# One attention branch's masked softmax: where its mask is added, and the order of its steps

## The reference, cut to what matters

```python
p_c = masked_softmax(jnp.einsum('bqghd,bcgd->bghqc', qn, kc_blk), cmp_end[None, :] <= t[:, None])
o_c = jnp.einsum('bghqc,bcgd->bqghd', p_c, vc_blk)
...
def masked_softmax(s, mask):
    s = jnp.where(mask, s, -jnp.inf)
    m = jnp.max(s, axis=-1, keepdims=True)
    m = jnp.where(jnp.isfinite(m), m, 0.0)
    e = jnp.exp(s - m)
    den = jnp.sum(e, axis=-1, keepdims=True)
    return e / jnp.where(den > 0.0, den, 1.0)
```

## Time and profile before

| what | value |
|---|---|
| median of 3 runs | 2557.27 us (2555.11 to 2559.82) |
| profiled execution | 2556.63 us, of which the traced span is 2554.8 us |
| PE busy | 2360.6 us (92%) |
| DVE / ACT / POOL busy | 1002.7 / 739.9 / 160.7 us |
| mean granted TensorE clock | 0.935 of full speed |
| the stage of the change | 1913.5 to 1942.4 us of the span, about 29 us, 1.1% |

### The profile page before, as it was taken

One profiled execution on the slowest core, in us unless ns is written; L12 is line 12 of the kernel. 1 busy time (PEld: TensorE's weight loads), 2 busy tenths in 40 slices (PEclk: granted clock), 3 DMA queues, 4 the chain that ended last, 5 costly groups with the idle time before them and its releaser, 6 DMA issues. The chain is left out here.

```text
span 2554.8 us, 35043 instructions
## 1 busy us (share of the span) xinstructions
PE 2360.6 (92%) x15098; PEld 1797.8 (70%) x15098; DVE 1002.7 (39%) x1684; ACT 739.9 (29%) x1249; POOL 160.7 (6%) x195
## 2 busy tenths in 40 slices
PE   6999999889999999984889999999987998999997
PEld 3545555768888778884767888877855556788885
DVE  2022365343333338553134433423336662442333
ACT  2124212232222224222223422322103562431331
POOL 0004100000000000022000000000022440000000
PEclk8999999899999989985589999998996998999999
DMA  7140014012132122000021222212110004122210
GB/s 298 66 189 34 1 68 166 34 66 99 66 130 76 43 99 99 34 34 4 2 99 66 99 99 99 99 69 99 68 34 1 1 2 165 66 99 99 99 66 33
DMA packets 17130, 196.23 MB, mean 77 GB/s; under 512 B 2000, under 2 KB 3152, under 8 KB 5072
## 3 DMA queue, kind: packets, MB, share of 16 engines
q1 hardware_dynamic: 15824, 189.67, 20.0%
q10 hardware_dynamic: 1152, 4.32, 0.4%
HBM read 189.78 MB, written 2.10 MB: 75 GB/s over the span
## 5 line engine op out<-in xcount | busy, mean ns | idle before, releaser
L1701 DVE TENSOR_TENSOR wsp_mlp<-ring,wsp_mlp 128x1024 fp32r<-128x1024 f32 x128 | 156.8, 1225 | 438.2 <-ACT wsp_mlp L1663 438.2
L1663 ACT CAST wsp_mlp<-ring 128x1024 fp32r<-128x1024 f32 x128 | 134.3, 1049 | 349.4 <-PE psum L1648 345.0
L1645 PE MATMUL psum<-hs_mlp,wsp_mlp 128*128 128x512 f32 x512 | 201.6, 394 | 8.1 <-DVE hs_mlp L1534 8.1
L1645 PE MATMUL psum<-acts_mlp,wsp_mlp 128*128 128x512 f32 x512 | 202.4, 395 | 0.0
L1647 PE MATMUL psum<-hs_mlp,wsp_mlp 128*128 128x512 f32 x512 | 201.2, 393 | 0.0
L1648 PE MATMUL psum<-hs_mlp,wsp_mlp 128*128 128x512 f32 x512 | 201.0, 393 | 0.0
L1648 PE MATMUL psum<-acts_mlp,wsp_mlp 128*128 128x512 f32 x512 | 199.4, 389 | 0.0
L1647 PE MATMUL psum<-acts_mlp,wsp_mlp 128*128 128x512 f32 x512 | 199.3, 389 | 0.0
L1701 DVE TENSOR_TENSOR wsp_ffn<-ring,wsp_ffn 128x1024 fp32r<-128x1024 f32 x66 | 80.9, 1225 | 237.3 <-ACT wsp_ffn L1663 237.3
L427 PE MATMUL psum<-hsev,wspev 128*128 128x512 f32 x672 | 157.2, 397 | 3.9 <-DVE wspev L407 3.9
L427 PEld LDWEIGHTS psum<-hsev,wspev 128*128 128x128 f32 x672 | 128.9, 192 | 31.9 <-DVE wspev L407 4.7
(11 more groups left out here) (427 smaller groups left out, 3984.3 us busy)
## 6 DMA issues: line engine op xcount, KB each, us to landing
ring<-weights SPq DMA_DIRECT2D x85, 2048.0 KB, 8.1
ring<-weights SPq DMA_DIRECT2D x3, 1024.0 KB, 5.2
xT<-xin SPq DMA_DIRECT2D x2, 1024.0 KB, 6.8
cst<-consts ACTq DMA_DIRECT2D x1, 1921.0 KB, 13.5
ring<-weights SPq DMA_DIRECT2D x1, 1280.0 KB, 6.6
mixT<-ctxin ACTq DMA_DIRECT2D x1, 1024.0 KB, 15.4
ring<-weights SPq DMA_DIRECT2D x2, 512.0 KB, 3.6
arena<-arena_low SPq DMA_DIRECT2D x8, 128.0 KB, 2.3
```

The costliest lines, as they stand in the source:

```text
L1645: pe.matmul(tile_bank(g, j), w_hi, src[:, 0, k0 + i, :], start=(first and i == 0), stop=False)
L1663: act.copy(wsp[:, q % 2, 0, :], raw_view(q)).then_inc(s["w_hi"], 1)
L1701: dve.tensor_tensor(wsp[:, q % 2, 1, :], raw_view(q), wsp[:, q % 2, 0, :].bitcast(F32), ALU.subtract).then_inc(s["w_lo"], 1)
```

## The change

- PE starts each score bank with a matmul of the identity and the mask row (broadcast to 8 heads, 248 columns), `start=True`; the 16 score matmuls then accumulate onto it. A tile's two banks now lie side by side (2i and 2i + 1), and `cmp_tile(i)` reads both as one operand.
- DVE's four mask additions go. The maximum is taken from PSUM; a new small instruction lifts it to at least `NEG / 2`, so that a row that is masked whole gives exp of a very large negative number, that is zero, and the product with `cmp_ok` goes, with its table of constants. The subtraction reads PSUM and writes `pc`.
- DVE's order is now `less_max(0)`, `less_max(1)`, `share(0)`, `less_max(2)`, `share(1)`, `less_max(3)`, `share(2)`, `share(3)`, where `less_max` is maximum, floor and subtraction, and `share` all that follows the exponential.
- `pc` has four buffers, so the wait for the transposes goes. POOL zeroes column 31 alone; PE waits for it (`cs_edge`) ahead of its transposes.
- ACT's copies now stand between the exponentials: exp(0), exp(1), copy(0), exp(2), copy(1), exp(3), copy(2), copy(3). On PE all scores still stand ahead of all transposes.

The diff:

```diff
@@ -122,7 +122,6 @@
     end = np.arange(32)[None, None, :] * CMP_STRIDE + CMP_BLOCK - 1
     ok = (end <= t) & (np.arange(32)[None, None, :] < NB_CMP)
     out["cmp_neg"] = np.where(ok, 0.0, NEG).astype(f32).reshape(P, TT * 32)
-    out["cmp_ok"] = ok.astype(f32).reshape(P, TT * 32)
     out["eighth"] = np.full((P, 1), 0.125, f32)
     out["one"] = np.ones((P, 1), f32)
     return out
@@ -2662,75 +2661,95 @@
         n6.close()
 
 
-        pc = sb("pc", [P, 2, NH, 32], n3)
+        pc = sb("pc", [P, TT, NH, 32], n3)
         cst8 = sb("cst8", [P, TT, 4, NH], n3)
         n4 = ExitStack()
         pcT = hT[:, 0:4, :]
-        cs_done, cs_sub, cs_exp, cs_prob, cs_turn, cs_out = (
-            sem(n) for n in ("cs_done", "cs_sub", "cs_exp", "cs_prob", "cs_turn", "cs_out"))
+        cs_done, cs_sub, cs_exp, cs_prob, cs_turn, cs_edge = (
+            sem(n) for n in ("cs_done", "cs_sub", "cs_exp", "cs_prob", "cs_turn", "cs_edge"))
+
+        def eights(ap):
+            return ap.rearrange("p (a x) -> p a x", a=2)
+
+        def cmp_tile(i):
+            both = psum.rearrange("p (b a n) -> p b a n", a=2, b=4)[:, i, :, 0:256]
+            return both.rearrange("p a (x n) -> p a x n", n=32)[:, :, :, 0:31]
+
+        def cmp_probs(i):
+            return pc[:, i, :, 0:31].rearrange("p (a x) n -> p a x n", a=2)
+
         with nc.Block() as block:
             @block.tensor
             def _(pe):
-                def cmp_scores(i):
+                for i in range(TT):
+                    for a in range(2):
+                        shut = C("cmp_neg", 32 * i, 31).rearrange("p (o n) -> p o n", o=1).to_broadcast([P, 8, 31])
+                        pe.matmul(cmp_tile(i)[:, a], ident, shut, start=True, stop=False)
                     for h in range(NH):
                         g, j = h // 4, h % 4
                         rows = slice(64 * (g % 2), 64 * (g % 2) + 64)
 
-                        at = 512 * (i + 4 * (g % 2)) + (4 * (g // 2) + j) * 32
+                        at = 512 * (2 * i + g % 2) + (4 * (g // 2) + j) * 32
                         last = pe.matmul(psum[:, at:at + 31], qT[rows, 4 * (g // 2) + j, i * P:(i + 1) * P],
-                                         kcb[rows, (g // 2) * 31:(g // 2) * 31 + 31], start=True, stop=True)
+                                         kcb[rows, (g // 2) * 31:(g // 2) * 31 + 31], start=False,
+                                         stop=(g >= 2 and j == 3))
                     last.then_inc(cs_done, 1)
-                for i in range(TT):
-                    cmp_scores(i)
+                pe.wait_ge(cs_edge, 1)
                 for i in range(TT):
                     pe.wait_ge(cs_prob, i + 1)
                     for g in range(NG):
-                        last = pe.transpose(bank(i)[:, g * P:(g + 1) * P],
-                                            pc[:, i % 2, 4 * g:4 * g + 4, :].rearrange("p a b -> p (a b)"), ident)
+                        at = 8 * (g % 2) + 4 * (g // 2)
+                        last = pe.transpose(bank(2 * i)[:, g * P:(g + 1) * P],
+                                            pc[:, i, at:at + 4, :].rearrange("p a b -> p (a b)"), ident)
                     last.then_inc(cs_turn, 1)
+
+            @block.gpsimd
+            def _(pool):
+                pool.memset(pc[:, :, :, 31], 0.0).then_inc(cs_edge, 1)
 
             @block.vector
             def _(dve):
                 link = chain(dve, "cmp_chain")
-                link(dve.memset(pc[:, :, :, :], 0.0))
+
+                def col(i, k):
+                    return cst8[:, i, k, :]
+
+                def wide(i, k):
+                    return eights(col(i, k)).rearrange("p a (x o) -> p a x o", o=1).to_broadcast([P, 2, 8, 31])
+
+                def less_max(i):
+                    dve.wait_ge(cs_done, i + 1)
+                    link(dve.tensor_reduce(eights(col(i, 0)), cmp_tile(i), AX.X, ALU.max))
+                    link(dve.tensor_scalar(col(i, 0), col(i, 0), NEG / 2, None, ALU.max))
+                    dve.tensor_tensor(cmp_probs(i), cmp_tile(i), wide(i, 0), ALU.subtract).then_inc(cs_sub, 1)
+
+                def share(i):
+                    dve.wait_ge(cs_exp, i + 1)
+                    link(dve.tensor_reduce(eights(col(i, 1)), cmp_probs(i), AX.X, ALU.add))
+                    link(dve.tensor_scalar(col(i, 2), col(i, 1), 0.0, None, ALU.is_equal))
+                    link(dve.tensor_tensor(col(i, 1), col(i, 1), col(i, 2), ALU.add))
+                    link(dve.reciprocal(col(i, 2), col(i, 1)))
+                    by_head = gates[:, i, 0:48:3].rearrange("p (x a j) -> p a x j", a=2, j=4)
+                    link(dve.tensor_tensor(col(i, 3).rearrange("p (a x j) -> p a x j", a=2, j=4),
+                                           col(i, 2).rearrange("p (a x j) -> p a x j", a=2, j=4), by_head, ALU.mult))
+                    dve.tensor_tensor(cmp_probs(i), cmp_probs(i), wide(i, 3), ALU.mult).then_inc(cs_prob, 1)
+
+                less_max(0)
                 for i in range(TT):
-                    e = pc[:, i % 2, :, 0:31]
-
-                    def row(name, n=NH):
-                        return C(name, 32 * i, 31).rearrange("p (o n) -> p o n", o=1).to_broadcast([P, n, 31])
-
-                    def col(k):
-                        return cst8[:, i, k, :].rearrange("p (h o) -> p h o", o=1)
-                    dve.wait_ge(cs_done, i + 1)
-                    if i >= 2:
-                        dve.wait_ge(cs_turn, i - 1)
-                    for g in range(NG):
-                        s = bank(i + 4 * (g % 2))[:, 128 * (g // 2):128 * (g // 2) + P]
-                        last = dve.tensor_tensor(e[:, 4 * g:4 * g + 4, :],
-                                                 s.rearrange("p (h n) -> p h n", n=32)[:, :, 0:31],
-                                                 row("cmp_neg", 4), ALU.add)
-                    link(last)
-                    link(dve.tensor_reduce(cst8[:, i, 0, :], e, AX.X, ALU.max))
-                    dve.tensor_tensor(e, e, col(0).to_broadcast([P, NH, 31]), ALU.subtract).then_inc(cs_sub, 1)
-                    dve.wait_ge(cs_exp, i + 1)
-                    link(dve.tensor_tensor(e, e, row("cmp_ok"), ALU.mult))
-                    link(dve.tensor_reduce(cst8[:, i, 1, :], e, AX.X, ALU.add))
-
-                    link(dve.tensor_scalar(cst8[:, i, 2, :], cst8[:, i, 1, :], 0.0, None, ALU.is_equal))
-                    link(dve.tensor_tensor(cst8[:, i, 1, :], cst8[:, i, 1, :], cst8[:, i, 2, :], ALU.add))
-                    link(dve.reciprocal(cst8[:, i, 2, :], cst8[:, i, 1, :]))
-                    link(dve.tensor_tensor(cst8[:, i, 3, :], cst8[:, i, 2, :], gates[:, i, 0:48:3], ALU.mult))
-                    dve.tensor_tensor(e, e, col(3).to_broadcast([P, NH, 31]), ALU.mult).then_inc(cs_prob, 1)
+                    if i + 1 < TT:
+                        less_max(i + 1)
+                    share(i)
 
             @block.scalar
             def _(act):
                 for i in range(TT):
                     act.wait_ge(cs_sub, i + 1)
-                    e = pc[:, i % 2, :, 0:31]
-                    act.activation(e, e, ACT.Exp).then_inc(cs_exp, 1)
-                for i in range(TT):
-                    act.wait_ge(cs_turn, i + 1)
-                    act.copy(pcT[:, :, i * P:(i + 1) * P], bank(i).rearrange("p (g n) -> p g n", g=NG))
+                    act.activation(cmp_probs(i), cmp_probs(i), ACT.Exp).then_inc(cs_exp, 1)
+                    if i >= 1:
+                        act.wait_ge(cs_turn, i)
+                        act.copy(pcT[:, :, (i - 1) * P:i * P], bank(2 * i - 2).rearrange("p (g n) -> p g n", g=NG))
+                act.wait_ge(cs_turn, TT)
+                act.copy(pcT[:, :, (TT - 1) * P:TT * P], bank(2 * TT - 2).rearrange("p (g n) -> p g n", g=NG))
 
 
         n2.close()
```

## The result

The changed kernel is slower. Six runs of each: median 2568.52 us (2564.8 to 2571.56) against 2556.19 us (2554.14 to 2560.0); ratio 1.0046, interval 1.0033 to 1.0059. Both intervals say slower.

A forecast was written before the change was run, and what follows sets the result against it. It took the clock slices to bound the span and DVE's chain the stage; with PE becoming the bound at half clock, the stage's +0.5 us and the constants' 0.2 saved gave +0.3: median 2557.6 us, range 2552.5 to 2562.

The forecast's parts named there:

- DVE's work: On DVE in the stage: a tile without waits costs 3.91 us instead of 5.9, 15.6 for four against 23.6.
- The clock: On PE in the stage: the clock falls again at about 1914.9 and stays at 0.50 while masks and scores run.
- The mask passes: On PE: each tile's two mask matmuls run as two passes each, 0.41 us a pass at half clock, 1.65 a tile.
- A tile at half clock: On PE: scores 3.46 us, masks 1.65 and identity loads 0.1 make 5.2 us a tile, more than DVE's 3.9.
- The second rival: On PE: score passes lose their overlap by adding onto a written bank, 3.4 us a tile longer, 2571 us; chance 5%.
- Tile 0: On PE: the first tile's masks and slower score passes add 1.5 us, so it comes at 1918.4.
- Tile 3: On PE: the last tile comes at 1934.0, three tiles of 5.2 us behind the first.
- From tile 3 to the end: DVE, ACT and PE behind the last tile's scores: 8.9 us to the last copy, with 0.8 lost waiting for exp(2).
- The sum: For the whole stage at clock 0.50: last copy ends at 1942.9 against 1942.41 before, 0.5 us longer.
- a side case: Next stage: it starts at another point against the clock, within 1 to 3 us; among the others, chance 4%.
- The range: For the whole time: 2552.5 to 2562 us, allowing 2 us by which runs differ.

The follow-up runs named there:

- e3: The changed kernel with all eight mask matmuls first on PE, then the 64 score matmuls in one stream: stage 26.89 us, ratio 0.9992 to the kernel before.
- e9: The changed kernel with each mask matmul on half the rows, the half that makes its bank's scores: stage 26.18 us, ratio 0.9977 to the kernel before.
- e4: The changed kernel with the order of before on DVE and ACT, masks still by PE: stage 29.57 us, ratio 1.0010 to the kernel before.
- e5: The changed kernel measured again as it is: median 2565.77 us against 2559.99 for the kernel before, ratio 1.0024.
- e1: The changed kernel with the 128 columns of cmp_ok kept unused in the constants' table: median 2567.92 us against 2561.39 for the kernel before.

## Why the prediction was wrong

It said 2557.6 us, range 2552.5 to 2562, and no change at 80%; the result is 2568.5, slower. The step that failed is the price of a tile on PE at half clock: 5.2 us by the sum, 6.43 measured. Step by step:

- **DVE's work**: right. `less_max` takes 1.6 us, `share` 2.3, the maximum from PSUM 0.68. DVE's busy time in the stage fell from 20.7 to 14.4 us, as forecast (6 to 7 less). A tile without a wait was put at 3.9 us; e3, where DVE waits for no scores behind the second tile, has 3.71.
- **The clock**: right for this order of PE's work. It fell 1.4 us in and stayed at 0.50 through 23 us in which PE was busy without a gap. The Trainium skill's section on the clock gate ("TensorE: Matmul & The Clock Gate", Part 1) would have one expect full clock after sustained work; this trace does not agree with it. e3 does, in one place: wide passes with no scores among them brought the clock back to 1.00 at 1916.5.
- **The mask passes**: right, 0.413 us each at half clock.
- **A tile at half clock, 3.46 + 1.65 + 0.1 = 5.2 us**: this is the step that failed. It took the score stream's price out of a stream without breaks, and allowed 0 to 0.4 us for the identity's loads. Measured are 6.43: 1.65 for masks, 0.30 for handovers, 4.48 for scores. The four score passes at either end of a tile start 0.21 to 0.24 us apart, that is alone, and only those between them in pairs. Our reading is that a pair is one pass from each of two neighbouring groups of heads, which use different halves of the array, and that the full-height masks keep a tile's first and last half group from finding a partner; the rows do not name the half, but four is half of a group's eight passes. That the height of the masks is the cause is shown: e9, which halves it and keeps the number of matmuls and columns, gives 4.35 us a tile, and e3, without masks between the tiles, 0.11 us a pass. The second rival had this mechanism, but as all or nothing (3.4 us a tile, 5%) and for a wrong reason, the accumulation.
- **Tile 0**: +4.9 us from the stage's start by the sum, +5.35 measured: here too the last four passes run alone. Tile 3: +20.5 by the sum, +24.65 measured: 0.45 + 3 x 1.23.
- **From tile 3 to the end**: 8.9 us and 0.3 to the next stage by the sum, 9.2 in all; 8.78 measured, with exp(2) behind copy(0) and its wait of 0.58, as described.
- **The sum** so gave +0.5 us for the stage; it was +4.25: 4.2 more up to tile 3, 0.4 less behind it. Added to that is 1.24 in the next stage, which the prediction held for 1 to 3 us in a side case. It follows from where the clock comes back: 13.2, 15.7 and (e4) 7.5 us behind that stage's start, with the first store at 28.41, 29.65 and 25.99: half a us for each us at 0.50.
- **The range**: it took 2 us for the difference between runs, from three runs within 5 us. The kernel before spread over 2540.58 to 2567.01 us in 35 runs. So the range held too little for this. The change's own part by the profiles is 4.25 + 1.24 = 5.5 us, up to 6.9 with what lies behind; e5's comparison gives 6.1 (1.8 to 10.5) and e1's, the same program but for the table, 6.7. The 12 us of the first comparison are that and, by the profiles, 5 us ahead of the stage which e5's profile does not have. That the first six runs differ by that much more is put down to such stretches by their profiles alone; the other runs of that set were not looked into.

Left open: the 1.4 us behind the next stage. The span's end came 440.5 to 440.8 us behind the last store in the changed kernel, e1 and e5, against 439.4 before, but 439.6 to 441.8 in the others, so no cause is named.

## What to carry to other kernels

Price work that is put into a stream by what the stream does around it: here small matmuls on half the rows ran two at a time, and two full-height matmuls (four passes) per tile cost 1.3 us beside their own 1.65. Ask first which engine a move makes the bound: moving the mask, 0.9 us a tile, off DVE put 3 us a tile on PE, which then set the pace, and the new order on DVE and ACT, good where DVE is late, became a cost of 2 us behind the last tile. And where most of a masked tile is known to be shut or open, try leaving the columns out first: here it gave a stage of 20.3 us, against 24.8 or more with each way of masking all of them.

## What the runs showed of the hardware

- Passes of 64 rows and 31 columns: 0.11 us each in one stream at clock 0.50, 0.14 with two full-height matmuls after every 32 passes; four passes at either end of a tile started 0.21 to 0.24 apart, that is alone.
- Masks on half the rows ran beside score passes: a tile 2.08 us shorter with the same number of matmuls and columns. Two mask passes of the next tile started ahead of this tile's last score pass, which the program has first (e9, 1932.06 and 1932.63 against 1932.69).
- Accumulating onto an opened bank costs a score pass nothing that these show (0.11 us a pass in e3, as before).
- The clock was at 0.50 through 23 us of PE busy without a gap, and came back in e3 while wide mask passes alone ran. Stretches early in the program ran at 0.50 in one run and near 1.00 in another of the same program, which moved all that follows by 14.7 us in sum.
- DVE read maxima over 112 to 496 columns across two PSUM banks in one instruction, 0.27 to 0.67 us; 496 columns from SBUF took 0.67 too.
